# A two-layer diffusion backbone in fp32: the boundaries between half-layers, and the prologue, in another order

## What is computed

```python
def rmsnorm(x, g):
    return x * rsqrt(mean(x * x, axis=-1) + 1e-6) * g

def sandwich_update(x, y_mix, mod, g, w1, w2):
    x = x + mod[2] * rmsnorm(y_mix, g[1])
    h = rmsnorm(x, g[2]) * (1 + mod[4]) + mod[3]        # scale, shift
    return x + mod[5] * rmsnorm(square(relu(h @ w1)) @ w2, g[3])
```

## Time and profile before

| | |
|---|---|
| three runs | 1463.76, 1463.84, 1466.75 us; median 1463.84 |
| the profiled execution | 1466.13 us, span 1464.4 |
| TensorE busy | 1368.5 us, 93% |
| VectorE, ScalarE, GpSimd busy | 894.8 (61%), 618.0 (42%), 120.8 us (8%) |
| mean granted clock | 0.971 |
| distance of two unit products at 2.4 GHz | 0.227 us |

### The profile page before, as it was taken

The page is one execution under the profiler, slowest core; times in us unless marked ns, Lnnn a source line. Parts: engine busy times, 40 slices in busy tenths (PEclk is TensorE's granted clock), DMA queues, the critical chain, the costliest instruction groups (busy, mean ns, idle before and its releaser), DMA issues. The chain is left out here.

```text
span 1464.4 us, 18029 instructions
## 1 busy us (share of the span) xinstructions
PE 1368.5 (93%) x6614; PEld 1127.9 (77%) x6614; DVE 894.8 (61%) x1291; ACT 618.0 (42%) x918; POOL 120.8 (8%) x149
## 2 busy tenths in 40 slices
PE   7889998999899999999988998899989999999996
PEld 2467787988688888888868887787768888888884
DVE  7668768987665554555456899988355333333333
ACT  4545445664362332514435334333445234252441
POOL 1661120002000000000110000000100000000011
PEclk9999999999899999999989999999989999999998
DMA  9434341118256565565322122221312323232221
GB/s 366 166 139 173 94 147 49 44 33 312 93 173 205 178 203 191 185 205 176 98 75 61 70 86 87 87 80 37 118 41 87 101 94 106 88 100 100 86 86 58
DMA packets 49417, 178.48 MB, mean 122 GB/s; under 512 B 5991, under 2 KB 8359, under 8 KB 46920
## 3 DMA queue, kind: packets, MB, share of 16 engines
q1 hardware_dynamic: 46344, 164.51, 33.4%
q0 software_dynamic: 3008, 13.11, 2.8%
HBM read 164.49 MB, written 10.49 MB: 119 GB/s over the span
## 5 line engine op out<-in xcount | busy, mean ns | idle before, releaser
L1706 PE MATMUL bank<-hhi,whi 128*128 128x512 f32 (+1 forms) x936 | 351.8, 376 | 10.3 <-ACT scratch L962 5.6
L1708 PE MATMUL bank<-hhi,wlo 128*128 128x512 f32 (+1 forms) x936 | 349.2, 373 | 0.0
L1707 PE MATMUL bank<-hlo,whi 128*128 128x512 f32 (+1 forms) x936 | 349.0, 373 | 0.0
L1098 DVE TENSOR_TENSOR wlo<-raw,whi 128x1024 fp32r<-128x1024 f32 x180 | 222.9, 1239 | 94.6 <-ACT whi L682 93.4
L682 ACT ACTIVATE whi<-raw 128x1024 fp32r<-128x1024 f32 x180 | 189.6, 1054 | 214.4 <-PE bank L1708 199.4
L1706 PE MATMUL bank<-ghi,whi 128*128 128x512 f32 x576 | 225.0, 391 | 4.7 <-DVE glo L1631 2.8
L1707 PE MATMUL bank<-glo,whi 128*128 128x512 f32 x576 | 224.8, 390 | 0.0
L1708 PE MATMUL bank<-ghi,wlo 128*128 128x512 f32 x576 | 224.6, 390 | 0.0
L1706 PEld LDWEIGHTS bank<-hhi,whi 128*128 128x128 f32 x936 | 176.3, 188 | 42.1 <-ACT whi L682 9.9
L1708 PEld LDWEIGHTS bank<-hhi,wlo 128*128 128x128 f32 x936 | 176.3, 188 | 31.2
L1707 PEld LDWEIGHTS bank<-hlo,whi 128*128 128x128 f32 x936 | 176.4, 188 | 30.5
(11 more groups left out here) (259 smaller groups left out, 1993.6 us busy)
## 6 DMA issues: line engine op xcount, KB each, us to landing
raw<-in_wpack SPq DMA_DIRECT2D x180, 512.0 KB, 3.4
araw<-in_apack SPq DMA_DIRECT2D x40, 512.0 KB, 3.4
amore<-in_apack SPq DMA_DIRECT2D x36, 512.0 KB, 3.4
ablk<-in_ahead SPq DMA_DIRECT2D x8, 1024.0 KB, 12.6
spectra<-scratch SPq DMA_DIRECT2D x16, 512.0 KB, 3.2
araw<-spectra POOLq DMA_DIRECT2D x8, 1024.0 KB, 5.1
fs<-in_fw SPq DMA_DIRECT2D x2, 1024.0 KB, 11.1
x<-in_xT SPq DMA_DIRECT2D x1, 2048.0 KB, 13.5
```

The lines of the kernel that those rows point to most:

```text
L1098: TT(wlo[:, s, :], raw[:, r, :], f(whi[:, s, :]), ALU.subtract).then_inc(lo_done, 1)
L1706: mm(o, lh, rh, start=first, stop=False)
L1707: mm(o, lh, rl, start=False, stop=False)
L1708: return mm(o, ll, rh, start=False, stop=last)
```

## The change

**The first four units of a boundary** (b < 3) no longer wait for x's norm. Their operand is g*x, x times the gain, made as soon as a group of two chunks is added: high part on ScalarE into `ghi`, low part on VectorE into `glo`. Norm and shift are linear in the output, so VectorE multiplies each of the four outputs by the spread inverse norm when it takes it from the bank (`first_evac`), and a column, the unit's weights times the shift vector, is added in ScalarE's ReLU, or in Hyena by an extra pass. The column comes from `shift_column`: products of 128x128 weights with two columns, 16 to a unit, and a small sum on VectorE. Unit 4 and those behind it use the normed, shifted operand as before, now in pieces of 512 tokens.

**x's squares** go to GpSimd, six additions of 128x512 at each of three boundaries, and TensorE makes columns of them as it does of y. x's rows are copied out of PSUM by ScalarE. y is scaled and added in four groups of two chunks; the last boundary stores 8 whole chunks, not 16 halves.

**The prologue** has another order: quarter 1 later, quarters 2 and 3 behind tile 7 with their low parts in other tiles, the table's split behind tile 5, all output sums ahead of the squares, four tiles for the four squares, and GpSimd's three additions in one place. **Filled waits**: two products more at the start, and three twice at the last boundary, whose results are not used. On SP the modulation's rows come one place later among the weights.

```diff
+            def boundary(b):                                   # TensorE
+                if b < 3:
+                    pe.wait_ge(shift_lo, b + 1)
...
+                    shift_column(b, 0, range(0, 4))
+                else:
+                    keep_busy(3)
                 pe.wait_ge(yacc_done, (KC - 2) * (b + 1))
-                square_column(S[:, 11, :], True, False)
+                square_column(B2[:, 0:QT], S[:, 11, :], True, False)
                 pe.wait_ge(ysq_done, KC * (b + 1))
...
+                if b < 3:
+                    shift_column(b, 0, range(4, KC))
+                else:
+                    keep_busy(3)
                 root_rows(b)
+                if b < 3:
+                    shift_column(b, 1, range(KC))
+                    shift_column(b, 2, range(KC)).then_inc(shiftcol_done, 1)
...
+            def shift_column(b, i, ks):
+                for k in ks:
+                    w = slice(k * P, (k + 1) * P)
+                    mm(SHIFTS[:, 2 * i:2 * i + 2], whi[:, i, w], shs[:, k, :], start=k == 0, stop=False)
+                    ins = mm(SHIFTS[:, 2 * i:2 * i + 2], wlo[:, i, w], shs[:, k, :], start=False, stop=k == KC - 1)
...
             def first_units(b):
-                x_sums(b, 0)
-                x_rows(b, 0)
-                x_sums(b, 1)
...
+                for k in range(5):
+                    pe.wait_ge(first_lo, KC * b + k + 1)
+                    for i in range(FIRST):
...
+                        products(i, (k,))
+                pe.wait_ge(first_lo, KC * (b + 1))
+                products(0, (5, 6, 7)).then_inc(unit_done, 1)
+                x_columns(b)
+                products(1, (5, 6))
+                x_rows(b)
+                products(1, (7,)).then_inc(unit_done, 1)
+                products(2, (5, 6, 7)).then_inc(unit_done, 1)
+                products(3, (5, 6, 7)).then_inc(unit_done, 1)
+                pe.wait_ge(shift_done, 2 * b + 1)
+                shift_column(b, 3, range(KC)).then_inc(shiftcol_done, 1)
...
+                unit(u0 + FIRST, 0, FIRST_BANKS[FIRST], hhi, hlo,
+                     lambda k: pe.wait_ge(h_done, operand_base(b) + k + 1), u0).then_inc(unit_done, 1)
```

```diff
+                group(0)                                       # VectorE, boundary
+                first_part(0)
+                prep(u0 + 3, 3, 1)
+                first_part(1)
+                group(1)
+                first_part(2)
+                group(2)
+                first_part(3)
+                group(3)
+                shift_sums(0, 3)
+                for j in range(4, KC):
+                    first_part(j)
+                dve.wait_ge(xroot_done, b + 1)
+                nc.vector.reciprocal(xroot[:, :], xroot[:, :]).then_inc(xinverse_done, 1)
+                prep(u0 + 4, 0, 0)
+                dve.wait_ge(xspread_done, b + 1)
+                for j in range(KC + 1):
+                    if j < KC:
+                        scaled_part(j)
+                    if j:
+                        low_part(j - 1)
+                    if j == 3:
+                        first_evac(b, 0)
...
             def x_square(i):                                   # ScalarE, prologue
                 if i >= 2:
-                    act.wait_ge(xadd_done, i - 1)
-                A(XSQ[:, min(i, 1), :], x[:, 2 * i:2 * i + 2, :].rearrange("p a n -> p (a n)"),
-                  ACT.Square).then_inc(xsq_done, 1)
+                    act.wait_ge(tlo_done, 1)
+                A(XSQ[i], x[:, 2 * i:2 * i + 2, :], ACT.Square).then_inc(xsq_done, 1)
...
+            def x_sums(b):                                     # GpSimd
+                for j in range(1, KC - 1):
+                    pool.wait_ge(xsquare_done, X_GROUPS * b + j // 2 + 1)
...
+                    nc.gpsimd.tensor_tensor(S[:, 11, :], S[:, 11, :] if j > 1 else y[:, 0, :], y[:, j, :],
+                                            ALU.add).then_inc(xacc_done, 1)
```

More of the change, by code:

```diff
@@ L1059, in _ @@
                     hy_prep(19)
-                for i in range(n + 2, n + 6):
+                for i in range(n + 2 if k else 7, n + 6):
                     hy_unit(i)
@@ L1264, in _ @@
             dve.wait_ge(tlo_done, 1)
-            for n in range(4, 8):
-                filter_tile(n)
-            filter_outs(0)
+            filter_tile(6)
+            filter_tile(7)
+            weight_sums(2)
+            weight_sums(3)
+            filter_out(0, 0)
+            weight_los(2)
+            modulation(0)
+            filter_out(0, 1)
+            weight_los(3)
             prep(0, 0, 0)
-            modulation(0)
             filter_outs(1)
@@ L1460, in boundary, with scaled_part, low_part @@
+                def scaled_part(j):
+                    STT(y[:, j, :], x[:, j, :], gcol(lo_, no_, j), XSPREAD, ALU.mult, ALU.mult).then_inc(ht_done, 1)
+                def low_part(j):
+                    dve.wait_ge(hhi_done, operand_base(b) + j + 1)
+                    STT(hlo[:, j, :], y[:, j, :], shift(ls, ts, j), f(hhi[:, j, :]), ALU.add,
+                        ALU.subtract).then_inc(h_done, 1)
                 if b == 3:
+                    for i in range(X_GROUPS):
+                        group(i)
@@ L1488, in quarter @@
                 for j in range(8):
-                    if not first or j:
+                    if not first or j >= 4:
                         prep(u0 + j + AHEAD, (j + AHEAD) % 4, (j + AHEAD) % 2)
+                    if first and j < 2:
+                        first_evac(2 * l, j + 2)
                     dve.wait_ge(ghi_done, c0 + j + 1)
@@ L1609, in hy_prep @@
                 prep(u, u % 4, u % 2)
-            for n in range(4):
-                if n:
-                    hy_prep(n)
-                hy_unit(n)
+            taps(0)
+            first_evac(1, 2)
+            taps(1)
+            first_evac(1, 3)
+            taps(2)
+            taps(3)
             def z_los(k):
@@ L1745, in ada_columns @@
                                         cst[0:2, 0, 0:2]).then_inc(acol_done, 1)
+            for i in range(2):
+                mm(B3[0:FH, :], S[0:NFEAT, 10, 0:FH], S[0:NFEAT, 6, :], start=True, stop=True)
             pe.wait_ge(silu_done, 1)
@@ L1986, in quarter @@
                     first_units(2 * l)
-                for j in range(3 if first else 0, 8):
-                    unit(u0 + j, j % 4, AB[:, j % 2, :], hhi, hlo).then_inc(unit_done, 1)
+                for j in range(FIRST + 1 if first else 0, 8):
+                    unit(u0 + j, j % 4, AB[:, j % 2, :], hhi, hlo,
+                         evacs=u0 + 2 if first and j < 7 else None).then_inc(unit_done, 1)
                 for j in range(8):
@@ L2054, in _ @@
             transposes(0)
[L2055 removed]
+            hy_unit(6)
             forward(0, 0)
[L2057 removed]
+            hy_unit(7)
             forward(0, 1)
[L2059 removed]
+            for n in range(8, 10):
                 hy_unit(n)
```

384 lines of the change are left out of this document (203 added, 181 removed).

## The result

The changed kernel takes **1477.47 us** (median of 4, 1475.44 to 1480.11) against 1465.3 us of the kernel before, measured beside it: 1.0083 times as long, 95% interval 1.0060 to 1.0106. It is slower by 12 us; the forecast was 10 us faster, and 1477 lies outside its range. The profiled execution took 1480.11 us, of which 1478.3 are its span, 13.9 more than the span before.

The account below looks back on a forecast made before the run. TensorE, busy 93% of the span, was taken as the bound, with VectorE setting Hyena's stretch. Terms -13.0 -1.8 +5.0 +0.0 +0.0 = -9.8 gave 1456.3 profiled, carried over to 1454.0 us; range 1439 to 1462.

Parts of the forecast that it names:

- TensorE does not wait before the column sums, so the first 8 cost 0.97: Boundary into an MLP: eight shift products ahead of the column sums cost only their own 0.97 us.
- I take R = Z+5.5: Boundary into an MLP: VectorE's first row scaling moves from 3.8 to 5.5 us behind the earlier kernel's column-sum start.
- R: At each boundary, the moment of VectorE's first row scaling, from which later times are counted.
- Z: At each boundary, the start of the column sums in the kernel before: 371.91, 747.40 and 1073.15.
- it is wrong if the granted clock is full through the shift products: Boundaries: sign that would refute the forecast, which expected 1.2 GHz and 0.2 us each for shift products behind R.
- The first rival: Boundaries: shift products hold the clock and sharing is small; 6.0 us more off per MLP boundary, 4.5 at Hyena's; 1437.5; chance 0.15.
- The terms behind R: MLP boundary: first product R+6.5, unit 0's end R+24.5, normed operand R+30.2, unit 4's end R+45.2, unit 7's R+63.0.
- Hyena's +5.0: Boundary into Hyena: VectorE sets the stretch, first inverse at R+101.3 = Z+106.8, 5.0 us later; bounds +3.5 to +7.
- 13 forecast: Prologue: reordering removes waits, first transform near 48 and fourth near 75, 13.0 us gained; bounds 9 and 15.5.
- I take the first, since the engine no longer stands still before it: Prologue: filling makes the first modulation block run at the later pace, ending 0.9 us earlier, otherwise 1.8 later.
- The rival on the slow side: Three boundaries: GpSimd's additions exclude VectorE's PSUM operations too, lengthening VectorE's chain, +13.8 us; 1471; chance 0.05.
- the point of R+26: Boundaries: VectorE's longer chain decides once the last unnormed operand is later than this; the forecast had it at R+21.3.

Follow-up runs that it names:

- e3: Changed kernel with TensorE's column sums moved ahead of every shift product and no wait for the shift's split ahead of them: 1462.92 us, 0.9997 of the kernel before.
- e4: e3 with the 48 shift products of units 0 to 2 moved behind the first products of chunks 1 to 3: 1463.79 us, 1.0003 of the kernel before.
- e7: Changed kernel, order kept, with eight unused 512-column products ahead of the wait for the shift's split: 1470.92 us, 1.0052 of the kernel before.
- e8: e3 with the column sums of x's squares ahead of unit 0's last nine products, x's rows behind them: 1460.65 us, 0.9986 of the kernel before.
- e9: e8 with x's sums ahead of chunk 4's products, rows three products later, unit 4's weights prepared behind the normed operand's first parts: 1452.21 us, 0.9924.
- e5: e3 without GpSimd's six additions of x's squares per boundary, x's norm taken from two of eight chunks: 1461.69 us, 0.9983 of the kernel before.
- e10: e9b with the boundary into Hyena and Hyena's first stage as in the kernel before: 1446.92 us, 0.9878 of the kernel before.
- e9b: e9 without the prologue's two filling products: 1453.16 us, 0.9929 of the kernel before.
- e1b: Kernel before with the new prologue alone, without its two filling products: 1455.30 us, 0.9945 of the kernel before.
- e1: Kernel before with the new prologue alone, its two filling products included: 1457.69 us, 0.9962 of the kernel before.

## Why the prediction was wrong

**The step that failed** is one sentence: "TensorE does not wait before the column sums, so the first 8 cost 0.97". The first half is true of the kernel before, but the change puts products there that need the shift, and the trace of before had the answer: VectorE finishes the modulation at 372.35, 0.7 us behind the last product at 371.67. I had costed the products and never asked when their operand is ready. From it followed "I take R = Z+5.5". With Z, the sums of before, at the same place, R came 3.7, 5.7 and 4.9 us later than that, 14.3 in sum, out of the 23.7 by which the forecast missed the profiled execution (4.6 more are the prologue's, 4.8 lie in the stretches behind R and at the end). Of the 14.3, 0.5 and 0.8 have another reason: Z+5.5 was worked out from R = Z+3.8 of the first boundary, and in the kernel before R stood at Z+4.4 and Z+4.6 at the other two. e3 shows the step: with the order changed and nothing else, 12.6 us come back in the timed runs.

**Inside that step** the half clock was priced for the shift products behind R, where it costs nothing that shows (e4), and half for the root's rows, but neither for the column sums nor for the eight shift products behind them, where it costs R: the sums take 2.81, 3.57 and 3.57 us instead of 1.95, 2.25 and 1.95. The wait and the eight products push the sums into or behind the fall of the clock; that the wait itself brings the clock down, e7 does not show. The sign "it is wrong if the granted clock is full through the shift products" did not come: from 367 on the clock is at half, and only the first eight products ran at full clock. The first rival (the boundaries pay too) falls with it.

**The terms behind R** held up. First boundary, measured against predicted, from R: first product 6.4 against 6.5; normed operand's start 32.7 against 30.2, its length 14.4 against 14.5; unit 4's end 48.1 against 45.2; unit 7's end 65.1 against 63.0. At Hyena the first inverse is at R+102.6 against R+101.3. Of the 2.5 us by which the operand starts late, 1.6 lie ahead of x's column sums, which start at R+26.1 and not at R+24.5. The other 0.9 are x's chain: its sums, its root and then unit 4's weights stand in a row ahead of the operand, and I had let the weights' preparation run beside it. e8 and e9 show that this chain and its place, and not GpSimd (e5), are what could be shortened.

**Hyena's +5.0** came out as +13.4. Of it 5.7 are R's delay beyond Z+5.5, and what remains, 7.7, is what e8 has there against before (333.3 to 325.7 us) with R nearly where it was: VectorE's additional work and its wait for unit 4's weights. e10, which undoes it, takes 6.3 off e9b. Direction and mechanism were right; the size was 1.5 times what was forecast.

**The prologue** gave 8.4 us in the trace and 5.6 in the timed runs (interval 2.9 to 8.2), against 13 forecast and 9 as the lower bound. Up to 2.7 us of it are the filling: "I take the first, since the engine no longer stands still before it" was wrong, the passes stayed at their slow pace. The other 2 to 4 us are VectorE's: the first transform without the filling starts at 49.8, not 47.7, and the fourth at 78.9, not 75.0, with two waits of 1.56 and 2.12 us ahead of it (TensorE in e1b):

```profile
75.46 0.50 PE L1778 MATMUL bank<-fw,fh 128*128 128x512 f32 x1 [1.56 <-DVE fs L1214]
...
78.92 0.77 PE L1712 MATMUL bank<-ghi,thi 128*128 128x512 f32 x1 [2.12 <-DVE scratch L1231]
```

The table's low part behaved (4.08 us); the sums of quarters 2 and 3 (1.09 to 1.78 us each in the changed kernel, where the earlier trace rows has 0.68 for one alone) and the tiles behind GpSimd's low parts took longer than I had placed for them.

**The rival on the slow side** had the sign and the size of a loss (1471) but the wrong mechanism: leaving GpSimd's additions out saves 2 us in all, not told from nothing (e5). The last unnormed operand was at R+23.5, short of the point of R+26 from which it should decide. 0.05 for everything on the slow side was too little, since the one rival there was built on an unknown price and not on the question that stood open, when each new product's operand is ready.

**Two slips in the working** did not decide anything. The upper bounds of the terms (-9, +1, +7, +2.5 and +1) add up to +2.5, so the sum of the bounds ends at 1466 and not at 1464; 1477 is outside either. And the earlier trace rows shows less than was read from it: of its digits only those of the four boundaries are below 9, the first slices and Hyena's are not.

## What to carry to other kernels

When a change puts new work of the bounding engine ahead of something urgent, find the producer of each of its operands in the trace of before and compare its end with the moment at which the engine arrives; a cheap product that waits costs its wait, and everything behind it. Then split the change: here one order (the sums first), and x's sums and one preparation moved, turned a loss of 12 us into a gain of 11 (e9), and with one of three boundaries left as it was the gain is 18 (e10). Where two engines take turns, work that one saves the other (Hyena's boundary) has to be read on the engine that sets that stretch.

## What the runs showed of the hardware

- Products with one or two columns did not keep TensorE's clock up. In the changed kernel, with 1.6 to 2.6 us without work just ahead, it fell to 1.2 GHz during them, and it came back only behind 5 to 6 us of 512-column products (from 379.14 to 384.2 at the first boundary). In e7, with no wait left at two boundaries, it fell all the same. It also fell in the changed kernel at 401.2, right behind x's column sums (16 one-column products in 1.95 us from 398.89), after 7.9 us without a wait:

```profile
400.60:401.20 0.60, 0.60 (x5) 0.56 (x5) 0.03 (x1) 0.33 (x2) 0.00 (x0) 1.00 0.00 0
401.30:401.90 0.60, 0.60 (x3) 0.51 (x2) 0.04 (x1) 0.60 (x1) 0.00 (x0) 0.50 0.00 0
```

- A short run of them does not always bring it down: the 16 shift products of unit 3, from 409.42 to 411.1 in the changed kernel, stand 0.11 us apart throughout. The Trainium skill, "TensorE: Matmul & The Clock Gate", What's actually happening, ties the clock to how busy the engine has been. The rows do not contradict it, and add that a stream of such small products, with no gap, ran at 0.50 from 367 to 379.
- A product of two columns against 128x128 weights takes 0.11 us from start to start at full clock and 0.21 at half.
- In the first 12 to 16 us of the program a pass of the first block takes 0.85 us and later 0.43, the ratio of the two levels. The views print a clock of 1.00 there, but the trace's record of the clock begins only later, with the full level, at 13.54 in e1b, 14.46 in e1 and 15.53 in the changed kernel. Each is within the pass in which the pace changes. So 1.00 at the start means that nothing is recorded, and the pace is that of 1.2 GHz. Filling products that kept the engine busy from 4.8 us on did not bring that moment forward: it lies between 12.6 and 15.6 in the eight traces with them, and between 12.2 and 14.1 in the four without.
